# Adding the last expert's rows by a one-hot product, gathering outputs ahead of the end, and a straight expert loop

## What is computed

```python
lg = h @ w_rg + b_rg                       # 4 groups, top 1
le = (h @ w_re + b_re)[chosen group]       # 8 experts of the group, top 2
weights = p_grp * top_p                    # two weights per token
y_e = (silu(x_e @ w_gate[e]) * (x_e @ w_up[e])) @ w_down[e]     # 32 experts, 1024 -> 512 -> 1024
f[token] = sum over its two experts of weight * y_e[row of token]
x = x + m5 * f;  then RMS norm of x        # next layer's first norm, or the final one
```

## Time and profile before

| | |
|---|---|
| median of 3 runs | 1980.71 us (1980.24 to 1982.86) |
| the profiled execution | 1979.41 us, its span 1977.6 us |
| PE busy | 1739.6 us (88%) |
| DVE, ACT, POOL busy | 681.4, 520.9, 155.4 us |
| DMA in the two MoE stages | 420 to 421 GB/s in most slices |

### The profile page before, as it was taken

One profiled execution on the slowest core, in us unless ns is written; L12 is line 12 of the kernel. 1 busy time (PEld: TensorE's weight loads), 2 busy tenths in 40 slices (PEclk: granted clock), 3 DMA queues, 4 the chain that ended last, 5 costly groups with the idle time before them and its releaser, 6 DMA issues.

```text
span 1977.6 us, 27111 instructions
## 1 busy us (share of the span) xinstructions
PE 1739.6 (88%) x9433; PEld 1009.5 (51%) x9434; DVE 681.4 (34%) x1444; ACT 520.9 (26%) x1061; POOL 155.4 (8%) x190
## 2 busy tenths in 40 slices
PE   5999899989985998999998599989968999988884
PEld 2766565668754443344443387778833333322222
DVE  4465255445544111111110565574551111111103
ACT  4344444442331110101111354452321101111011
POOL 0063031000000000000000215230000000000000
PEclk8999999999987999999999799999988999999997
DMA  8346565323337999999999433234499999999993
GB/s 321 133 170 224 187 224 184 131 66 96 111 158 292 366 420 421 421 420 421 421 421 420 175 124 100 88 113 135 134 370 371 422 421 421 420 421 421 420 421 132
DMA packets 96052, 550.59 MB, mean 278 GB/s; under 512 B 14162, under 2 KB 15650, under 8 KB 42724
## 3 DMA queue, kind: packets, MB, share of 16 engines
q1 hardware_dynamic: 83108, 526.89, 67.2%
q0 software_dynamic: 4224, 11.35, 2.0%
q10 hardware_dynamic: 8640, 11.28, 1.6%
HBM read 537.15 MB, written 12.32 MB: 278 GB/s over the span
## 4 chain that ended last, share of the span: by engine, by line
PE 64%; DMA 15%; DVE 7%; SPq 6%; ACT 4%; issue 4%; POOL 0%; ACTq 0%; POOLq 0%; DVEq 0%
PE ps L825 14%; DMA moe<-in_w_exp_gate_up_dram 11%; PE ps L541 8%; PE ps L840 8%; PE ps L543 8%; PE ps L542 8%; SPq L466 5%; PE ps L809 3%; PE ps L760 2%; PE ps L687 2%; PE ps L716 2%; PE ps L698 2%; DMA moe<-in_w_mod_dram 1%; DMA moe<-in_w_exp_down_dram 1%; DVE w_lo L1354 1%
## 5 line engine op out<-in xcount | busy, mean ns | idle before, releaser
L825 PE MATMUL ps<-moe,ht 128*64 128x512 f32 x1600 | 369.2, 602 | 60.5 <-DMA moe<-in_w_exp_gate_up_dram 38.2
L1710 DVE TENSOR_TENSOR arena<-arena,ps 128x256 f32<-128x256 f32 x64 | 27.0, 422 | 714.1 <-ACT arena L1254 714.1
L825 PEld LDWEIGHTS ps<-moe,ht 128*64 128x64 f32 x1600 | 110.8, 138 | 309.8 <-issue 237.7
L541 PE MATMUL ps<-ht_hi,w_hi 128*128 128x512 f32 (+1 forms) x704 | 252.4, 359 | 2.0 <-ACT arena L1143 1.6
L543 PE MATMUL ps<-ht_hi,w_lo 128*128 128x512 f32 (+1 forms) x704 | 243.7, 346 | 0.0
L542 PE MATMUL ps<-ht_lo,w_hi 128*128 128x512 f32 (+1 forms) x704 | 243.5, 346 | 0.0
L1354 DVE TENSOR_TENSOR w_lo<-ws,w_hi 128x1024 fp32r<-128x1024 f32 (+1 forms) x122 | 149.2, 1228 | 223.1 <-ACT w_hi L1048 223.0
L840 PE MATMUL ps<-moe,arena 128*64 128x512 f32 x960 | 219.7, 598 | 1.1
L1048 ACT ACTIVATE w_hi<-ws 128x1024 fp32r<-128x1024 f32 (+1 forms) x122 | 125.2, 1026 | 175.8 <-PE ps L543 146.4
L541 PEld LDWEIGHTS ps<-ht_hi,w_hi 128*128 128x128 f32 x704 | 133.3, 189 | 24.4 <-issue 9.0
L543 PEld LDWEIGHTS ps<-ht_hi,w_lo 128*128 128x128 f32 x704 | 133.1, 189 | 16.9
(11 more groups left out here) (263 smaller groups left out, 2143.5 us busy)
## 6 DMA issues: line engine op xcount, KB each, us to landing
moe<-in_w_exp_gate_up_dram SPq DMA_DIRECT2D x200, 1024.0 KB, 20.8
moe<-in_w_exp_down_dram SPq DMA_DIRECT2D x120, 1024.0 KB, 20.8
ws<-in_w_exp_gate_up_dram SPq DMA_DIRECT2D x48, 1024.0 KB, 26.5
ws<-in_w_in_dram SPq DMA_DIRECT2D x92, 512.0 KB, 4.1
moe<-in_w_mod_dram SPq DMA_DIRECT2D x29, 1536.0 KB, 6.6
y_rows<-arena ACTq DMA_DIRECT2D x164, 64.0 KB, 5.5
ws<-in_w_branch_dram SPq DMA_DIRECT2D x16, 512.0 KB, 3.5
ws<-in_w_out_dram SPq DMA_DIRECT2D x16, 512.0 KB, 3.5
```

The costliest lines, as they stand in the source:

```text
L541: pe.matmul(ps[:, bank, 0:cols], w[:, k, :], a_hi, start=(i == 0), stop=False)
L825: mm = pe.matmul(ps[BLK * j:BLK * j + BLK, 2, :].rearrange("p (g n) -> p g n", g=2), xg[:, k, BLK * s:BLK * s + BLK], places[k // 2][0][:, ...
```

## The change

1. PE's loop of groups has the four experts one after the other, with no inner loop of halves. In layer 0 the loop's first instruction is placed at slot 0 of a block of instructions.
2. The gathers no longer wait for the last expert's rows. ACT counts `rows_saved` once per expert, ahead of its silu, when the rows of the expert before are saved; POOL starts at count 32 of the layer. So that this can be counted, ACT's three waits for saves move from behind the silu to ahead of it.
3. `yg` lies in `moe` (places that the last expert does not use).
4. A token's assignment to main rows of expert 31 is taken out of the gathers (its index becomes 0, its weight 0). DVE builds `last_pick` (12 small operations, two of 128 x 512 or 256, once per layer), PE turns it after the last expert, DVE copies it to `last_rows`. In the tail PE multiplies `ysb` by `last_rows` (8 products of 128 columns per tile) and adds the gathered rows to the same banks by 8 products with the identity, where it made 8 transposes.
5. In the tail, ACT's root table load, `round_first` and DVE's `leave_first` stand later.

```diff
-        yg = [[part(base, at + 8 * i + 4 * k, 4) for k in range(2)] for base, at in ((arena, 16), (moe, 48)) for i in range(2)]
+        yg = [[part(base, at + 8 * i + 4 * k, 4) for k in range(2)] for base, at in ((moe, 0),) for i in range(3)] + [[part(moe, 64 + 4 * k, 4) for k in range(2)]]
+        last_pick, last_rows = part(ht_flat, 6, 2), part(arena, 44, 2)
...
-                with pe.Fori(0, QUADS) as four:
-                    with pe.Fori(0, 2) as half:
-                        with pe.If(half < 1):
-                            places = pieces_of(l, 0, four)
-                            overflow(FOUR * four, ("xg_set", gathered + 4 * four + 4), places)
-                            expert(FOUR * four, four, 0, places)
...
+                with nc.Fori(0, QUADS, engines=[mybir.EngineType.PE], head_slot={mybir.EngineType.PE: 0} if l == 0 else None) as four:
+                    for s in range(FOUR):
+                        places = pieces_of(l, s, four)
+                        overflow(FOUR * four + s, ("xg_held", QUADS * FOUR * l + 4 * four + s) if s
+                                 else ("xg_set", gathered + 4 * four + 4), places)
+                        expert(FOUR * four + s, four, s, places)
...
+                pe.wait_ge(g["last_set"].sem, g["last_set"].at(l))
+                for tile in range(nt):
+                    mm = pe.transpose(ps[:, 1, tile * P:(tile + 1) * P], last_pick[:, tile * P:(tile + 1) * P], ident[:, :])
+                mm.then_inc(g["last_turned"].sem, g["last_turned"].tick(l))
                 pe.wait_ge(g["y_copied"].sem, NE * (l + 1) + 1)
+                pe.wait_ge(g["last_copied"].sem, g["last_copied"].at(l))
...
+                    for c in range(KC):
+                        rows = slice(BLK * (c // 4), BLK * (c // 4) + BLK)
+                        pe.matmul(ps[:, banks[c // 4], (c % 4) * P:(c % 4 + 1) * P], ysb[rows, (c % 4) * P:(c % 4 + 1) * P],
+                                  last_rows[rows, tile * P:(tile + 1) * P], start=(c % 4 == 0), stop=False)
                     pe.wait_ge(g["comb"].sem, g["comb"].at(l, tile))
                     for c in range(KC):
-                        mm = pe.transpose(ps[:, banks[c // 4], (c % 4) * P:(c % 4 + 1) * P], hr[:, tile, c * P:(c + 1) * P], ident[:, :])
+                        mm = pe.matmul(ps[:, banks[c // 4], (c % 4) * P:(c % 4 + 1) * P], hr[:, tile, c * P:(c + 1) * P], ident[:, :],
+                                       start=False, stop=(c % 4 == 3))
...
+                    act.wait_ge(g["y_saved"].sem, done * 32 + 32)
+                    act.wait_ge(g["yt_saved"].sem, act.snap(n_tails, min_val=0, max_val=64) * 32 + 32)
+                    act.wait_ge(g["yo_saved"].sem, act.snap(n_more, min_val=0, max_val=64) * 64 + 64)
+                    act.nop(nofuse=True)
+                    act.sem_inc(g["rows_saved"].sem, 1)
                     act.wait_ge(g["gu_used"].sem, 4 * done + 4)
                     nc.scalar.activation(act_g, ps[:, 2, 0:256], ACT.Silu).then_inc(g["silu_done"].sem, 1)
-                    act.wait_ge(g["y_saved"].sem, done * 32 + 32)
-                    act.wait_ge(g["yt_saved"].sem, act.snap(n_tails, min_val=0, max_val=64) * 32 + 32)
                     act.wait_ge(g["down_used"].sem, 2 * done + 2)
                     nc.scalar.activation(ysb, ps[:, 4, :], ACT.Copy).then_inc(g["y_copied"].sem, 1)
                     act.wait_ge(g["y_copied"].sem, done + 2)
-                    act.wait_ge(g["yo_saved"].sem, act.snap(n_more, min_val=0, max_val=64) * 64 + 64)
...
-                pool.wait_ge(g["prep"].sem, g["prep"].at("y", l))
+                pool.wait_ge(g["last_set"].sem, g["last_set"].at(l))
+                pool.wait_ge(g["rows_saved"].sem, NE * (l + 1))
```

More of the change, by code:

```diff
@@ L264, in hybrid_block @@
         names = f"""ident_in mean_in consts_in rows_in_done vecs_in router_in swa_in wst0 wst1 wst2 wst3 wst4 wst5 mwt0 mwt1 mwt2 mwt3 mwt4 mwt5 cond_in bias0 bias1 bias2
-            bias3 {" ".join(f"gu_in{i}{j}" for i in range(2) for j in range(4))} {" ".join(f"spare_in{i}" for i in range(5))} wd_in00 wd_in01 wd_in10 wd_in11 y_saved yo_saved yt_saved yg_got0 yg_got1 yg_got2 yg_got3 out_saved
+            bias3 {" ".join(f"gu_in{i}{j}" for i in range(2) for j in range(4))} {" ".join(f"spare_in{i}" for i in range(5))} wd_in00 wd_in01 wd_in10 wd_in11 y_saved yo_saved yt_saved rows_saved last_set last_turned last_copied yg_got0 yg_got1 yg_got2 yg_got3 out_saved
             in_turned in_copied prep vec_ready cond_silu cond_turned cond_cols vecs_turned vec_cols sq_done sq_added mean_done rstd_sqrt
@@ L287, in apart, with pieces_of @@
             return (0, 1, 2) if l == 0 else (0, 1, 2, 3, 4)
-        def pieces_of(l, s, four, half=0):
+        def pieces_of(l, s, four):
             if s % 2:
-                turn = PAIRS * l + 2 * four + s // 2 + half + 1
+                turn = PAIRS * l + 2 * four + s // 2 + 1
                 return [(wgu[1][i], gu_in[1][i], turn) for i in range(4)] + [(wd[1][i], wd_in[1][i], turn) for i in range(2)]
@@ L1269, in _ @@
                         expert(2 * two + s)
[L1270 to L1273, removed]
                 after = (l + 1, "n1") if l + 1 < DEPTH else (l, "fin")
@@ L1285, in square_tile @@
                         .then_inc(g["sq_done"].sem, g["sq_done"].tick(*after, tile))
[L1287 to L1290, removed]
+                act.wait_ge(g["last_set"].sem, g["last_set"].at(l))
                 for tile in range(nt):
+                    if tile == 2 or nt == 2 and tile == 1:
+                        load_roots()
                     got = yg_got[tile]
@@ L1297, in _ @@
                         square_tile(tile - 2)
+                if l + 1 < DEPTH:
+                    round_first(l + 1)
+                act.wait_ge(g["y_saved"].sem, 32 * NE * (l + 1) + 32)
+                act.wait_ge(g["yt_saved"].sem, act.snap(n_tails, min_val=0, max_val=64) * 32 + 32)
                 for tile in range(nt - 2, nt):
@@ L1677, in _ @@
                 set_four(FOUR)
+                apart_k, kept = [tmp(1696, nt), tmp(1700, nt)], tmp(1704, nt)
+                w_apart, w_last = [tmp(1708, nt), tmp(1712, nt)], tmp(1716, nt)
+                for k in range(2):
+                    of_last = ohe[k][:, :, NE - 1:NE].rearrange("p t e -> p (t e)")
+                    chain(v.scalar_tensor_tensor(apart_k[k], pos_k[k], float(BLK), of_last, ALU.is_lt, ALU.mult))
+                    chain(v.tensor_scalar(kept, apart_k[k], -1.0, 1.0, ALU.mult, ALU.add))
+                    chain(v.tensor_tensor(dest_k[k], dest_k[k], pos_k[k], ALU.add))
+                    chain(v.tensor_tensor(dest[:, k, 0:nt], dest_k[k], kept, ALU.mult))
+                    chain(v.tensor_tensor(w_apart[k], route_w[:, k, 0:nt], apart_k[k], ALU.mult))
+                    chain(v.tensor_tensor(route_w[:, k, 0:nt], route_w[:, k, 0:nt], w_apart[k], ALU.subtract))
+                chain(v.tensor_tensor(w_last, w_apart[0], w_apart[1], ALU.add))
+                twice = last_pick[:, 0:nt * P].rearrange("p (t j n) -> p t j n", j=2, n=BLK)
+                chain(v.tensor_tensor(twice, place1[:, 0:nt, NE - 1:NE].unsqueeze(3).broadcast_to([P, nt, 2, BLK]),
+                                      slots1[:, 0:BLK].unsqueeze(1).unsqueeze(1).broadcast_to([P, nt, 2, BLK]), ALU.is_equal))
+                v.tensor_tensor(twice, twice, w_last.unsqueeze(2).unsqueeze(3).broadcast_to([P, nt, 2, BLK]), ALU.mult) \
+                    .then_inc(g["last_set"].sem, g["last_set"].tick(l))
                 if l == 0:
@@ L1746, in _ @@
                         add_tile(tile - 1)
+                if l + 1 < DEPTH:
+                    leave_first(l + 1)
                 add_tile(nt - 1)
```

20 lines of the change are left out of this document (2 added, 18 removed).

## The result

| | before | changed |
|---|---|---|
| median of 4 runs | 1980.75 us (1980.24 to 1982.86) | 2036.69 us (2034.67 to 2044.33) |
| profiled execution, its span | 1979.41, 1977.6 us | 2044.33, 2042.1 us |
| PE busy | 1739.6 us | 1789.7 us |

The ratio is 1.0287, 95% interval 1.0259 to 1.0315: the change makes the kernel 56 us slower, where 15 us faster was forecast.

What follows compares the result with a forecast made beforehand. Full DMA queues were taken to bound the MoE stages, plus times they ran dry. Terms -7.9 -5.1 +13 +1.5 +1.0 -9.9 -7.0 = -14.4 took 1979.4 to 1965.0; with that run 1.3 below the median, 1966 us, range 1952 to 1984.

Steps and rivals of the forecast that it cites:

- The straight loop: PE's expert loop in both MoE stages: the code-loading stall behind the first expert goes, -7.9 and -5.1 us.
- does not stay loaded: Rival, PE's loop: seven blocks and one ahead are too many, repeats wait for code; 35 us per layer, 2011; chance 0.08.
- The waits moved ahead of the silu: ACT in the MoE stages: saves and table loads make silus late, +13 us in layer 0, +1.5 in layer 1.
- all of it: Upper bound for the moved waits, with all of PE's lateness paid: +33 us in layer 0, +16 in layer 1.
- A four-piece save makes the silu 1.6 us late: MoE experts: last piece lands 1.5 us behind the silu, plus 0.1 for added instructions; the expert is as late.
- In DMA-bound stretches 2.2 us of slack per expert cover most of it: MoE stages: where DMA sets the pace, slack covers most lateness from saves and table loads; in PE-bound stretches nothing does.
- The tails: Behind each layer's last expert: earlier gathers and PE adds save 9.9 us in layer 1, 7.0 in layer 0.
- Full clock is my choice: Tails: PE assumed at full clock; at half rate each set takes 3.8 us and layer 1's gain is 2.
- Gathers beside the last weights: End of layer 1's stage: gathers sharing queues with the last down weights cost at most +1.0 us; nothing in layer 0.
- waits in full, tails at low clock: Rival: layer 0 pays 6 us more, tail 1 gives 2 and tail 0 gives 4; 1983 us, chance 0.14.
- the five: The rivals: waits covered 0.2, waits in full 0.14, loop not loaded 0.08, far jumps wait 0.02, fetch gap stays 0.06.
- The forecast's own test: Sign of being right: silus at +7.9 or +9.2 us behind the copy, where they stood at 6.3 in PE-bound stretches.

Runs made afterwards that it cites:

- e2: The straight PE loop alone put into the kernel before: 1971.39 us, ratio 0.9939.
- e9: Changed kernel with waits ahead of the silu in each layer's last expert alone, layer 0's loop head at slot 230 instead of 0: 2058.64 us, ratio 1.0394.
- e3: Changed kernel with the three waits and the count put back behind every silu: 1958.28 us, ratio 0.9884.
- e12: Changed kernel with table load ahead of the waits, PE filled with 14 transposes behind four-piece saves, loop heads at slot 0: 1985.55 us, ratio 1.0021.
- e5: Changed kernel with a one-column silu ahead of the waits, so that the table load stands ahead of them: 1989.14 us, ratio 1.0032.
- e15: Changed kernel with waits ahead in the last expert alone, plus twelve small activations between gate/up and every silu: 1987.66 us, ratio 1.0018.

## Why the prediction was wrong

The forecast was 1966 us, in a range of 1952 to 1984; it came to 2036.69. Point by point.

**The straight loop: right.** Said -7.9 and -5.1; `e2`'s trace has -7.9 and -5.3. The stall of 10.01 us is gone. What is left is two slow branches at the first jumps, of 2.1 and 4.9 us, and no slow back edge (ns min/median/max):

```profile
L897 PEldq COMPARE_BRANCH  x64: 77/208/4932, 616.7 to 1995.1; - x64
...
L927 PEldq COMPARE_BRANCH  x17: 76/208/333, 615.3 to 2009.7; - x17
```

The loop has 1639 instructions, where I had counted 1605, and six packets of code came between 612 and 664 us, where I had said about seven. That the loop stays loaded was right, but with more luck than I knew. I gave the rival "does not stay loaded" 0.08 and priced it by the number of blocks. I left out that the place of the head decides whether a loop of 6.4 blocks touches seven or eight, and took the fixed head for a detail; it is worth 103 us. The rival's price was too low too: 35 us per layer, where refetching in layer 0 alone cost 103 (`e9`). The Trainium skill (Runtime: NRT & Kernel Launch, "Instruction fetch mechanics") puts PE's store at 2048 instructions, eight blocks; here a loop over seven stayed, and one over eight only in some cases. Its rule that a taken branch out of a window of two pages waits for a fetch is not what this trace shows: the back edge at L927, 1639 instructions long in layer 0, took 333 ns at most.

**"The waits moved ahead of the silu": the step that failed.** It said +13 and +1.5; by `e3` against the changed kernel it is 67.9 us in layer 0 and 22.9 in layer 1 of the traces, 78 us in the medians, above even the bound I called "all of it", +33 and +16. The mechanism and its place were right, silu and table load behind the save, but a term was missing (the lower clock behind PE's longer waits) and the rest was sized too low. Four points:

1. The late silu was priced at its lateness. "A four-piece save makes the silu 1.6 us late" is nearly what `e12` shows with the table load and the clock taken away (15.0 against 13.2 us, 1.8). The trace of the kernel before had it too: its four-piece saves landed 8.1 to 8.2 us behind the copy, 1.9 behind the silu's 6.27, where I had worked out 1.5 from medians. But PE's longer waits have a second price, the 1.6 us of lower clock, in 24 experts some 38 us. Together with the table load, which I had added as 1.3 us on every second expert, and with saves that landed later, it made 4.9 us per four-piece expert (18.1 against 13.2); the 13 of layer 0 come to 64 us.
2. The parts do not just add. The table load is 1.28 us, and its move in `e5` gave 47 us, since with it PE waited longer in so many experts that the clock fell in 24 and not in 11. I had added costs that each make the other dearer.
3. "In DMA-bound stretches 2.2 us of slack per expert cover most of it" held while they were rare. At 1.40 us on every expert `e15` already lost 21 us in layer 0, about half of the 45 that 32 experts make; that the two overflow experts use up the reserve is my guess, and no run tests it. The window from 742 us on, DMA-bound before, ran at 368 GB/s.
4. The saves landed later than before: 6.3 us in the median between 820 and 1020 us, 7.7 at most, where the kernel before had 5.6 and 6.5. No run here shows why; the queues ran at 333 GB/s in the mean there, not at 421.

```profile
DMA to landing us min/median/max: 5.3/6.3/7.7
```

**The tails: right in kind, two thirds in size.** Layer 1, said E+16.2, -9.9:

```profile
2014.19 1.15 ACT L1287 ACTIVATE arena<-moe,route_w 128x1024 f32<-128x1024 f32 x1 [1.45 <-issue]
...
2016.71 2.05 PE L960 MATMUL ps<-ident,arena 128*128 128x128 f32 x16 [1.96 <-DVE arena L1755]
...
2022.42 2.16 DVE L1744 SCALAR_TENSOR_TENSOR xt<-ps,modv,xt 128x128 f32<-128x128 f32 x8 [1.14 <-PE ps L960]
...
2024.84 5.44 PE L945 MATMUL ps<-arena,mean_w 128*128 128x128 f32 x32 [2.45 <-DVE xt L1744]
```

With E = 2012.1 (the end of the last L841) the scaling is at E+2.1, the first identity product done at E+6.7, the adds at E+12.5: every step within 0.3 us of the sum. Only the norm's sums, said 3.8, took 5.44, with a clock of 0.63 (2024 to 2028 us) behind PE's 2.45 us of waiting for the adds: E+18.2. The earlier trace rows had shown them at 5.76 behind the same 2.45; I read the full-clock value from layer 0 instead. So -7.9. Layer 0, said -7.0: sums end at E+30.1 and not E+26.5, -3.4. The first 14 us of that tail in the changed kernel, and in `e5`, columns as above:

```profile
1155.00:1169.00 14.00, 11.98 (x66) 11.25 (x67) 6.61 (x13) 7.03 (x7) 6.65 (x7) 0.63 0.66 227
```

```profile
1115.00:1129.00 14.00, 12.43 (x111) 11.79 (x112) 10.62 (x27) 9.98 (x10) 6.40 (x7) 1.00 0.61 215
```

At 0.63 PE did 66 products in it, at 1.00 it did 111. `e5`'s last sums end 25.7 us behind its last down product, 0.8 earlier than said: "Full clock is my choice" was the term that failed, and the clock in this tail differs from trace to trace (`e12`: 0.70).

**Gathers beside the last weights: nothing lost.** Said +1.0. POOL's first gather ran at 2004.94, E-7.2 (said E-8), and the last copy ended 6.14 us behind the start of its silu, as before.

**The rival "waits in full, tails at low clock"**, at 0.14, was the nearest of the five, and was priced at 1983, because its waits in full were still lateness alone. The forecast's own test said silus at +7.9 or +9.2 us behind the copy. Behind four-piece saves in layer 0 they stood at +8.5 to +9.7, and with the table load at +9.8 to +10.9. The clock came on top of that lateness.

## What to carry to other kernels

Ask of a wait that is put ahead of a hand-over to PE not only how late it makes PE, but how long PE then idles at a time. Here idle times of up to 1.2 us cost no more than themselves; behind those of 2 to 3 us the clock fell in most rounds, at 1.6 us each, and behind all longer ones in the changed kernel's loops. If a count is needed once, take the wait once: a branch for the last round kept the early gathers, and the 31 other experts of the layer lost nothing. And for a loop that nearly fills the instruction store the place of its head can matter as much as its length: count the blocks that it touches, fix the head, and look at the packets of code in the trace.

## What I had not expected of the hardware

- A loop of 1639 PE instructions stayed loaded from slots 0 and 100 of a block of 256, and was refetched in each round from slot 230 and about 181: 53 and 54 packets of code against 117 and 116, 1955 and 1962 us against 2059 and 2058.
- One wait of 2.13 us at the same place left full clock behind it in one expert and a fallen clock (0.56 between 731.8 and 734.0 us) in the next four or five; waits of 2.61 us in layer 1 left it in only 20 of 32.
- A table load of 1.28 us, moved from behind the waits to ahead of them, was worth 47 us.
- Two DMA pieces of 64 rows landed no sooner than four of 32.
